# Front steps dealt out one by one to each engine, sample attention moved ahead of the last group, one choice of experts moved ahead of the front

## The chip, the cores and the metric

The kernel runs on one core of a Trainium2 chip. The metric is the device time of one execution in microseconds (us), the median of several runs. Engines: PE (TensorE, matrix products), DVE (VectorE), ACT (ScalarE), POOL (GpSimd, which issues the gathers here), SP (SyncE, which issues all other DMAs). Each engine works through its own instructions strictly in order; semaphores connect them.

## The reference

One layer over 1024 prompt tokens and 128 sample tokens (8 streams of 16), together nine tiles of 128 tokens, D = 1024:

```
h = rms_norm(x);  z = h @ w_in            # rq rk rv rg fq fk fv and forget gates
ro = retention(rq, rk, rv)                # 8 heads of 64, chunked recurrence
fo = fox attention(fq, fk, fv, logf)      # 8 heads of 64; samples also see 256 cached frames
x = x + concat(norm(ro)*silu(rg), norm(fo)) @ w_out
xn = rms_norm(x)
q = xn @ wq                               # 8 heads x 2 halves x 128
s1, s2 = q1 @ keys1, q2 @ keys2           # 128 scores each
v1,i1 = top16(s1); v2,i2 = top16(s2)
cv,ci = top16(v1[:,None] + v2[None,:])    # 16 of 256 pairs
e = i1*128 + i2;  g = softmax(cv)         # 128 experts per token (8 heads x 16)
x = x + sum(g * gelu(xn . u[e]) * v[e])   # u, v: 16384 x 1024 each
```

## The kernel before

Five programs follow one another: norm, a first projection, retention, a second projection, and the tail. Only the tail changes. It does, for each of the nine tiles of 128 tokens, 128 *gathers* (one per expert slot): gather n fetches for each of the 128 tokens a row of u and v (8 KB), 1 MB in all, into one of NR = 9 ring buffers. DVE multiplies the u half with the token's x and sums (a *dot*, L1701). After four dots DVE and ACT make the gelu weights (*weigh*, L1710 to L1723, with ACT's tanh at L1234, `gelu_tanh`), and PE adds four v halves with 16 matrix products into `yp` (*add_v*, L1458). That frees four ring buffers; POOL waits for it (`uv_free`) before it issues the next four gathers (L1068). Four dots and one add_v are a *block*; a tile has 32 blocks, the program 288. `replicate_x` on PE (L1446) and `spread_x` on ACT (L1230) copy a tile's x into the four rows of 32 that the dots read.

What a tile needs before its gathers is the *front*. The tiles go in three groups of three (g = 0, 1, 2; tile 8, the last of group 2, holds the samples). The front of a group has, in order:

- `load`: SP loads queries `fq`, keys `kTg`, values `vg`, decays `cB`, retention output `mix`
- `fox` m (24 in group 0 and 1, 16 in group 2): one head and one tile of prompt attention, scores on PE (L1275), a DVE pass (L1600), exp on ACT, transposes and values on PE; `fout` collects a pair of heads
- in group 2, sample attention: `sload` loads what it needs, `sprep` prepares on DVE, and nine rounds of `skeys`, `sscore`, `snorm` (PE L1328 to L1364, DVE L1631, L1636, ACT L1159), then `sback`
- `hload` to `hxt`: norms, the product with w_out (L1390), residual, second norm, transposes (L1400)
- `rq`, `rturn`, `rscore` i (12 per group): the product with wq (L1411), transposes (L1420), scores against the keys (L1429, semaphore `s_mm`); ACT copies each result; `rtop` i, p on DVE (L1507 to L1520) takes the top 16. Copy i of the scores on ACT waits for `top_done` of i - 2
- the *choice* of a tile, `rcand` i, p (31 pieces with work, L1527 to L1583, on DVE), then `rexp` on ACT (exp L1214, and 16 copies of the indices, L1122), `rgate` on DVE (L1691), `rmove` on ACT (16 copies of the gates). Gathers of tile t wait for its indices (`moved`).

The order of all this is fixed when the program is written. In before, `front_steps(g)` gives one list for all engines. Group 0's whole list runs before the first dot, with the choice of tile 0 after the four top-16 steps that it needs. `due_steps` spreads the lists of group 1 (behind the choices of tiles 1 and 2) and group 2 over blocks 0 to 191, by a rough cost on PE and DVE, and each engine does its share of a block's steps in that block. Gather 4 and all later ones also wait for the twelfth `rscore` of group 0 (`s_mm` 12), because the ring's buffers hold weights until then; gathers 0 to 3 do not.

The scratch area `S` is shared: in before the sample attention uses the parts that prompt attention used, so it must come after it. SP takes its share too, with the stores of y, the loads of x and `xTn` between the steps, in the same order.

## Time and profile before

| | |
|---|---|
| median of 3 runs | 4227.95 us (4224.69 to 4232.9) |
| the profiled execution | 4225.2 us, span 4223.3 us |
| first and last gather issued | 943.9 and 4202.9 us |
| moved by all DMAs | 1347.64 MB, of it 1208.03 MB by gathers |
| DVE, PE busy | 2497.4 us (59%), 2441.4 us (58%) |
| longest share of the chain that ended last | gathers, 18% of the span |

"DMA share" in the rows is how busy the 16 DMA engines were; the view shows 1.01 where they were never idle. The span falls into three parts: up to about 940 us the projections and group 0's front, then gathers beside the front of groups 1 and 2, and from about 3200 us gathers alone.

### The profile page before, as it was taken

How to read it: one execution, taken by the hardware profiler on the slowest of the kernel's cores; microseconds unless marked ns; L12 is line 12 of the kernel's file. 1: busy time of each engine (PE TensorE's matmuls, PEld its weight loads, DVE VectorE, ACT ScalarE, POOL GpSimd, SP SyncE). 2: the span in 40 equal slices, each digit the busy share in tenths (PEclk: the TensorE clock that was granted, in tenths of full speed). 3: DMA queues.
4: the chain of work that ended last, by engine and by line, in shares of the span. 5: the costliest groups of instructions: out<-in, count | busy, mean ns of one | idle time of the engine just before them, and what ended most of it. 6: DMA issues, size and time to landing. Idle time of an engine off the chain costs nothing. (4 is left out here: it accounts for less than half of the span.)

```text
span 4223.3 us, 34616 instructions
## 1 busy us (share of the span) xinstructions
PE 2441.4 (58%) x11906; PEld 1010.6 (24%) x11906; DVE 2497.4 (59%) x6235; ACT 478.1 (11%) x1311; POOL 1357.3 (32%) x1257
## 2 busy tenths in 40 slices
PE   7998996757338667533376766764334334334333
PEld 3465443323004223200033432221001001001000
DVE  3211720166956558999565454788985555555555
ACT  1000111221013111100022111111000000000000
POOL 0000220001433333444333233344444444444443
PEclk9966996778559889765588677987556556556555
DMA  3001034113999999999999799999999999999998
GB/s 107 20 10 52 20 117 151 74 40 137 415 365 387 388 386 417 403 410 411 415 415 399 303 374 394 376 405 406 420 416 418 419 416 412 419 417 418 422 418 371
DMA packets 241776, 1347.64 MB, mean 319 GB/s; under 512 B 33457, under 2 KB 47097, under 8 KB 94145
## 3 DMA queue, kind: packets, MB, share of 16 engines
q0 software_dynamic: 165888, 1208.03, 69.8%
q1 hardware_dynamic: 73408, 135.08, 8.8%
q10 hardware_dynamic: 2304, 2.32, 0.2%
q8 instruction: 94, 1.54, 0.1%
q14 instruction: 82, 0.66, 0.0%
HBM read 1318.14 MB, written 27.21 MB: 319 GB/s over the span
## 5 line engine op out<-in xcount | busy, mean ns | idle before, releaser
L1068 POOL DMA_INDIRECT M<-in_peer_uv,M x1152 | 1277.7, 1109 | 2069.8 <-PE yp L1458 1616.1
L1701 DVE SCALAR_TENSOR_TENSOR M<-M 128x1024 f32<-128x1024 f32 x1152 | 1407.3, 1225 | 650.9 <-DMA M<-in_peer_uv,M 616.9
L1458 PE MATMUL yp<-M,strips 128*32 128x512 f32 x4608 | 923.5, 945 | 1441.0 <-DVE strips L1723 1396.8
L1458 PEld LDWEIGHTS yp<-M,strips 128*32 128x32 f32 x4608 | 161.6, 147 | 2112.9 <-DVE strips L1723 1668.4
L332 PE MATMUL z<-M 128*128 128x512 f32 x1008 | 440.7, 594 | 1.4 <-PEq L104 1.0
L1234 ACT ACTIVATE gel<-gel 128x4 f32<-128x4 f32 x288 | 59.8, 208 | 1948.9 <-DVE gel L1712 1938.4
L1411 PE MATMUL ab<-M 128*128 128x512 f32 x576 | 271.0, 622 | 11.4 <-DMA M<-in_peer_wq 10.1
L332 PEld LDWEIGHTS z<-M 128*128 128x128 f32 x1008 | 189.0, 191 | 225.8 <-issue 225.8
L414 POOL TENSOR_SCALAR small<-small 128x8 f32<-128x8 f32 x27 | 6.1, 227 | 514.6 <-DVE small L483 514.6
L1411 PEld LDWEIGHTS ab<-M 128*128 128x128 f32 x576 | 111.2, 200 | 154.9 <-issue 153.3
L1600 DVE CUSTOM_DVE_ANT_0 M<-ab,M 128x896 f32<-128x896 f32 (+6 forms) x64 | 48.4, 758 | 155.9 <-PE ab L1277 88.2
L1275 PE MATMUL ab<-M 64*128 64x512 f32 (+3 forms) x192 | 97.5, 622 | 51.1 <-issue 28.3
L1723 DVE SCALAR_TENSOR_TENSOR strips<-gel,exg 128x128 f32<-128x128 f32 x288 | 84.0, 292 | 68.5 <-ACT gel L1234 59.3
L1446 PE MATMUL ef<-ident,M 128*32 128x128 f32 x2304 | 92.0, 290 | 17.3 <-issue 12.5
L1701 DVE DVE_READ_ACCUMULATOR M<-M 128x1 f32 x1152 | 95.4, 83 | 0.0
L1298 PE MATMUL d<-M 128*64 128x128 f32 x576 | 89.0, 306 | 10.9 <-ACT M L1116 10.9
L1718 DVE TENSOR_TENSOR exg<-e,gel 128x128 f32<-128x128 f32 x288 | 84.0, 292 | 10.0
L1390 PE MATMUL c<-M 128*128 128x512 f32 x144 | 75.4, 674 | 19.1 <-ACT M L1178 14.0
L1507 DVE MAX8 M<-M 128x8 f32<-128x128 f32 x144 | 31.3, 280 | 91.8 <-ACT M L1210 91.8
L1446 PEld LDWEIGHTS ef<-ident,M 128*32 128x32 f32 x2304 | 72.1, 118 | 52.0 <-issue 37.7
L1298 PEld LDWEIGHTS d<-M 128*64 128x64 f32 x576 | 70.0, 153 | 27.2 <-issue 26.6
L1429 PE MATMUL d<-M 128*128 128x128 f32 x288 | 45.1, 304 | 41.4 <-issue 22.4
(201 smaller groups left out, 2356.7 us busy)
## 6 DMA issues: line engine op xcount, KB each, us to landing
M<-in_peer_wq SPq DMA_DIRECT2D x12, 2048.0 KB, 28.5
M<-in_peer_uv,M POOLq DMA_INDIRECT x1152
M<-in_w_in SPq DMA_DIRECT2D x7, 2048.0 KB, 9.1
M<-in_w_out SPq DMA_DIRECT2D x24, 512.0 KB, 22.5
M<-in_x_prompt SPq DMA_DIRECT2D x16, 512.0 KB, 5.9
x_scratch<-M SPq DMA_DIRECT2D x9, 512.0 KB, 8.0
xts_scratch<-M SPq DMA_DIRECT2D x9, 512.0 KB, 20.9
M<-xts_scratch SPq DMA_DIRECT2D x9, 512.0 KB
```

What stands on the lines that cost most here:

```text
L332: last = nc.tensor.matmul(z[n % 3][:, :], hT[:, k, t * P:(t + 1) * P], wbuf[:, gi % 2, k, :], start=(k == 0), stop=(k == KC - 1))
L1068: nc.gpsimd.indirect_dma_start(ring[n % NR], None, a["peer_uv"], bass.IndirectOffsetOnAxis(ap=idxH[:, t % 6, s // 4, s % 4:s % 4 + 1], axis=0)
L1234: nc.scalar.activation(gel[:, n % 2, 2, :], gel[:, n % 2, 1, :], ACT.Tanh).then_inc(gel2, 1)
L1275: nc.tensor.matmul(s[:, c:c + w], fq[b0:b0 + 64, r, i * P:(i + 1) * P], kTg[b0:b0 + 64, r, c:c + w], start=True, stop=c + w < width)
L1298: last = nc.tensor.matmul(Dk[b0:b0 + 64, 0:P], vg[:, j, h * HD:(h + 1) * HD], pT[:, n % 2, j, :], start=(j == 0), stop=(j == t))
L1390: last = nc.tensor.matmul((C, Dk)[c][:, :], mT[:, t % 2, k, :], wout(g)[:, k, 512 * c:512 * c + 512], start=(k == 0), stop=(k == KC - 1))
L1411: last = nc.tensor.matmul(half_ab[i % 2], xT[:, tt, k, :], wq(g, b)[:, k, :], start=(k == 0), stop=(k == KC - 1))
L1446: last = nc.tensor.matmul(EF[32 * b:32 * b + 32, half, k * P:(k + 1) * P], xTn[:, 4 * half + k, 32 * j:32 * j + 32], ident[:, :], start=Tr ...
L1458: last = nc.tensor.matmul(yp[32 * j:32 * j + 32, 512 * c:512 * c + 512], strips[:, n % 2, j, :], ring[(4 * n + j) % NR][:, D + 512 * c:D + ...
L1701: nc.vector.scalar_tensor_tensor(out=row, in0=row, scalar=1.0, in1=xrep[:, s % 4, :], op0=ALU.mult, op1=ALU.mult, accum_out=dots[:, t % 2, ...
L1718: link(nc.vector.tensor_tensor(exg[:, :, :], bc(e32[:, :].unsqueeze(1), [P, 4, 32]), bc(g[:, 3, :].unsqueeze(2), [P, 4, 32]), ALU.mult))
L1723: nc.vector.scalar_tensor_tensor(out=strips[:, n % 2], in0=bc(g[:, 2, :].unsqueeze(2), [P, 4, 32]), scalar=1.0, in1=exg[:, :, :], op0=ALU. ...
```

## The change

`front_steps()` now gives each step its part on every engine, with a cost and the steps it must wait for, including who holds a PSUM bank. There are two lists (*threads*): all choices, and the rest. `deal` walks through time and gives each engine its next step or its next piece of expert work (dot, tanh, add_v, gather), whichever can start first; a step is placed ahead of expert work only if it ends by the time that work is ready, give or take a slack. When a choice and another step could start at once, the choice goes first. Each engine now has its own list of what stands before which dot (`due["dve"][n]`, n a dot), block (`due["pe"]`, `due["act"]`), gather (`due["pool"]`), or one of three places per tile (`due["sp"]`).

With that: group 0's steps end between the first dots, not before them. `spread` (tile 0's x) stands between the second and third `rq` of group 0. The choice of tile 1 stands in the middle of group 0's top-16 steps. `load` is split: keys, values and decays wait only for the last `rscore` of the group before, queries and `mix` (`loadq`) for the last gate. Sample attention comes before group 2's prompt attention, in parts of `S` that the scores and choices don't use; it has its own copy of the sample queries (`qs`), and `sload` waits only for group 1's last `rscore`. What is computed stays the same.

```diff
-        def front_steps(g):
-
-            nt, L = len(tiles_of(g)), FIRST[g + 1] - FIRST[g]
-            out = [(0, 0, "load", g)] + [(3.0, 0, "pad", g)] * (3 if g else 0)
-            for m in range(L + 3):
-                blocks = FOX[min(FIRST[g] + m, FIRST[g + 1] - 1)][2] + 1
-                out.append((0.7 * blocks, 0.3 + 0.13 * blocks, "fox", g, m))
-                if m >= 2 * nt + 2 and (m - 2) % (2 * nt) == 0:
-                    out.append((0.6, 0.7, "fout", g, (m - 2) // (2 * nt) - 1))
-            if nt < GT:
...
-            choice = [[(0, 1.15, "rcand", g, i, p) for p in range(CAND)] +
-                      [(0, 0, "rexp", g, i), (0, 0.6, "rgate", g, i), (0, 0, "rmove", g, i)] for i in range(GT)]
...
+
+            def add(thread, name, **parts):
+                thread.append((name, {e: (p[0], list(p[1:])) for e, p in parts.items()}))
+
+            def bank(names, engine, name):
...
+        def front_steps():
...
+            def add(thread, name, **parts):
+                thread.append((name, {e: (p[0], list(p[1:])) for e, p in parts.items()}))
...
+                chosen = [("dve", ("rgate", g - 1, GT - 1))] if g else []
+                if nt < GT:
+                    add(rest, ("sload", g), sp=(30.0, *routed))
+                    for p in range(3):
+                        add(rest, ("sprep", g, p), dve=(1.3, ("sp", ("sload", g))))
+                    for b in range(NB + 1):
+                        at = [("dve", ("snorm", g, b - 1)), ("dve", ("sscore", g, b - 1))] if b else []
+                        dead = [("pe", ("sscore", g, b - 1))] if b else []
+                        late = [("sp", ("sscore", g, b - 2))] if b >= 2 else []
+                        add(rest, ("skeys", g, b), pe=(3.2, *at, *late, ("sp", ("sload", g)), *bank("AB", "act", ("skeys", g, b))),
+                            act=(1.9, ("pe", ("skeys", g, b)), *dead))
+                        ready = [("act", ("skeys", g, b)), ("dve", ("sprep", g, 2))]
+                        ready += [("sp", ("snorm", g, b - 2))] if b >= 2 else []
+                        add(rest, ("sscore", g, b), sp=(20.0, ("pe", ("skeys", g, b))),
+                            pe=(5.0, *ready, *bank("C", "act", ("sscore", g, b))),
+                            dve=(1.0, ("pe", ("sscore", g, b))), act=(0.5, ("dve", ("sscore", g, b)), *at))
+                        add(rest, ("snorm", g, b), sp=(20.0, ("pe", ("sscore", g, b))),
+                            dve=(0.7, ("act", ("sscore", g, b)), ("pe", ("skeys", g, b))))
+                    add(rest, ("sback", g), pe=(1.2, ("dve", ("sscore", g, NB)), *bank("A", "act", ("sback", g))),
+                        act=(0.6, ("pe", ("sback", g))))
+                    routed = [("act", ("sback", g))]
+                add(rest, ("load", g), sp=(40.0 if g else 12.0, *routed))
+                add(rest, ("loadq", g), sp=(15.0, *chosen))
...
+                    if g == 0 and i == 2:
+                        add(rest, ("spread", g), pe=(5.0, ("sp", ("hxt", g, GT - 1))), act=(5.0, ("pe", ("spread", g))))
...
+                for i in range(GT):
+                    top = ("rtop", g, 4 * i + 3 if g == 0 else n - GT + i, 4)
+                    for p in range(CAND):
+                        add(choice, ("rcand", g, i, p), dve=(1.15, ("dve", top)))
+                    add(choice, ("rexp", g, i), act=(4.6, ("dve", ("rcand", g, i, CAND - 1))))
+                    add(choice, ("rgate", g, i), dve=(0.7, ("act", ("rexp", g, i))))
+                    add(choice, ("rmove", g, i), act=(4.2, ("dve", ("rgate", g, i))))
+            return choice, rest
...
-        def due_steps():
-
...
+        def deal(threads):
...
+            slack = {"pe": 2.5, "dve": 2.5, "act": 0.5, "pool": 2.0, "sp": 0.0}
+            count = {"pe": 32 * TILES, "dve": P * TILES, "act": 32 * TILES, "pool": P * TILES, "sp": 3 * TILES}
...
+            def step_start(e, th):
+                if at[e][th] == len(queue[e][th]):
+                    return None
+                need = queue[e][th][at[e][th]][1][e][1]
+                if any(d not in done for d in need):
+                    return None
+                return max([free[e]] + [done[d] + 0.1 for d in need])
...
+                if e == "pool":
+                    moved = done.get(("act", ("rexp", i // P // GT, i // P % GT)))
+                    if moved is None or i >= NR and (i - NR) // 4 >= len(freed):
+                        return None
+                    empty = done.get(("pe", ("rscore", 0, 4 * GT - 1)))
+                    if i >= 4 and empty is None:
+                        return None
+                    return max(moved, empty if i >= 4 else 0.0, freed[(i - NR) // 4] if i >= NR else 0.0)
+                if e == "dve":
+                    return None if i >= len(landed) else landed[i]
...
+            while True:
+                best = None
+                for e in engines:
+                    work = work_ready(e)
+                    bound = hoped(e) if work is None else work
+                    found = None
+                    for th in range(len(threads)):
+                        start = step_start(e, th)
+                        if start is None or found and found[0] <= start:
+                            continue
+                        cost = 0.1 if e == "sp" else queue[e][th][at[e][th]][1][e][0]
+                        if start + cost <= bound + slack[e]:
+                            found = (start, e, th)
+                    if found is None and work is not None:
+                        found = (max(work, free[e]), e, None)
+                    if found and (best is None or found[0] < best[0]):
+                        best = found
+                if best is None:
+                    break
+                start, e, th = best
+                i = did[e]
+                if th is not None:
+                    name, parts = queue[e][th][at[e][th]]
+                    at[e][th] += 1
+                    due[e][i].append(name)
+                    free[e] = start + (0.1 if e == "sp" else parts[e][0])
+                    done[(e, name)] = start + parts[e][0]
+                    continue
...
-            qbd = S[:, 0:1024].rearrange("p (r b a q) -> p r b a q", r=PAIRS, b=NB, a=2)
-            ckT = S[:, 1024:2048].rearrange("p (r n) -> p r n", r=PAIRS)
-            pn, pns = S[:, 2048:2320], S[:, 2320:2592]
-            psT = S[:, 2592:2976].rearrange("p (j m) -> p j m", j=3)
-            foT = S[:, 2976:3488].rearrange("p (r n) -> p r n", r=PAIRS)
-            kTs = S[:, 3488:4000].rearrange("p (r n) -> p r n", r=PAIRS)
-            e64 = S[0:64, 4000:5024].rearrange("p (b m) -> p b m", b=NB)
-            lfs, cs, ones_s = S[0:64, 5024:5296], S[0:64, 5296:5568], S[0:64, 5568:5840]
+            kTs = S[:, 0:512].rearrange("p (r n) -> p r n", r=PAIRS)
+            e64 = S[0:64, 512:1536].rearrange("p (b m) -> p b m", b=NB)
+            qs = S[:, 1536:2048].rearrange("p (r n) -> p r n", r=PAIRS)
+            qbd = S[:, 5904:6928].rearrange("p (r b a q) -> p r b a q", r=PAIRS, b=NB, a=2)
+            ckT = S[:, 6928:7952].rearrange("p (r n) -> p r n", r=PAIRS)
+            pn, pns = S[:, 7952:8224], S[:, 8224:8496]
+            psT = S[:, 8496:8880].rearrange("p (j m) -> p j m", j=3)
+            foT = S[:, 8880:9392].rearrange("p (r n) -> p r n", r=PAIRS)
+            lfs, cs, ones_s = S[0:64, 9392:9664], S[0:64, 9664:9936], S[0:64, 9936:10208]
...
-            due = due_steps()
+            due = deal(front_steps())
...
+                        w = (tiles_of(g)[-1] + 1) * P
                         if g:
-                            sp.wait_ge(q_mm, 4 * GT * g)
-                            sp.wait_ge(gate_done, GT * g)
-                        w, t0 = (tiles_of(g)[-1] + 1) * P, GT * g
-                        sp.dma_start(fq, a["qts"][:, :, t0 * P:(t0 + GT) * P]).then_inc(fq_in, 16)
+                            sp.wait_ge(s_mm, 4 * GT * g)
+                        if len(tiles_of(g)) < GT:
+                            sp.wait_ge(fT_ev, 1)
...
+                    elif kind == "loadq":
+                        t0 = GT * g
+                        if g:
+                            sp.wait_ge(gate_done, t0)
...
-                        sp.wait_ge(ofin, 4 * g + 4)
+                        sp.wait_ge(s_mm, 4 * GT * g)
                         sp.dma_start(kTs, a["kts"][:, :, NP_TOK:]).then_inc(sc_in, 16)
+                        sp.dma_start(qs, a["qts"][:, :, NP_TOK:]).then_inc(sc_in, 16)
...
-                for n in range(NR):
+                for n in range(P * TILES):
+                    for step in due["pool"][n]:
+                        front(step)
                     if n == 4:
                         pool.wait_ge(s_mm, 4 * GT)
                     gather(n)
-                for b in range(32 * TILES):
-                    for step in due[b]:
-                        front(step)
-                    for n in range(4 * b + NR, min(4 * b + NR + 4, P * TILES)):
-                        gather(n)

             @block.scalar
             def _(act):
...
-                for step in front_steps(0)[0]:
-                    front(step[2:])
-                dve.wait_ge(e32_in, 16)
                 for t in range(TILES):
                     for s in range(P):
+                        for step in due["dve"][t * P + s]:
+                            front(step)
+                        if t == 0 and s == 0:
+                            dve.wait_ge(e32_in, 16)
                         dot(t, s)
-                        for step in between(due[32 * t + s // 4], s % 4):
-                            front(step)
                         if s % 4 == 3:
                             weigh(t, s // 4)
                         if s == 2 and t >= 1:
                             finish(t - 1)
+                for step in due["dve"][P * TILES]:
+                    front(step)
```

DVE at the end of group 0's front, in before: the choice of tile 0 (L1581 its last piece, L1691 the gate) and the next top 16, then, after the last top (L1520), the first dot (L1701) with the choice of tile 1 (from L1527).

```order
L1581 SCALAR_TENSOR_TENSOR M<-M 128x128
L1583 TENSOR_TENSOR M<-M 128x128
L1687 TENSOR_REDUCE M<-M 128x8
L1688 RECIPROCAL small<-M 128x8
L1691 TENSOR_TENSOR gate<-M,small 128x128
L1507 MAX M<-M 128x8 x4
...
L1516 MAX M<-M 128x8 x4
L1520 MAX_INDEX M<-M 128x8 x4
L1701 SCALAR_TENSOR_TENSOR M,dots<-M 128x1024
```

The same place in the change (L1882 is the dot, L1697 and L1701 the end of a top 16, L1688 the start of one, L1708 to L1764 a choice, L1891 the weigh):

```order
L1697 MAX M<-M 128x8 x4
L1882 SCALAR_TENSOR_TENSOR M,dots<-M 128x1024
L1701 MAX_INDEX M<-M 128x8 x4
L1882 SCALAR_TENSOR_TENSOR M,dots<-M 128x1024
L1688 MAX M<-M 128x8 x4
L1882 SCALAR_TENSOR_TENSOR M,dots<-M 128x1024 x2
...
L1701 MAX_INDEX M<-M 128x8 x4
L1688 MAX M<-M 128x8 x4
L1708 CAST M<-M 128x256
...
L1762 SCALAR_TENSOR_TENSOR M<-M 128x128
L1764 TENSOR_TENSOR M<-M 128x128
L1692 MAX_INDEX M<-M 128x8
```

Dots 0 to 3 now stand around the end of the sixth top and the start of the seventh, and after the first row of top 9 (counted from 1) the whole choice of tile 1 stands before its second row.

DVE at the first dots of tile 6, in before (L1730 adds tile 5 to the output after tile 6's third dot; the first rows are the last weigh of tile 5):

```order
L1718 TENSOR_TENSOR exg<-e,gel 128x128
L1723 SCALAR_TENSOR_TENSOR strips<-gel,exg 128x128
L1701 SCALAR_TENSOR_TENSOR M,dots<-M 128x1024 x3
L1730 TENSOR_TENSOR M<-yp,M 128x1024
L1701 SCALAR_TENSOR_TENSOR M,dots<-M 128x1024
```

In the change, L1762 and L1764 are the last piece of the choice of tile 6, and L1868 to L1872 its gate:

```order
L1882 SCALAR_TENSOR_TENSOR M,dots<-M 128x1024
L1762 SCALAR_TENSOR_TENSOR M<-M 128x128
L1764 TENSOR_TENSOR M<-M 128x128
L1882 SCALAR_TENSOR_TENSOR M,dots<-M 128x1024
L1891 SCALAR_TENSOR_TENSOR gel<-dots 128x4
...
L1701 MAX_INDEX M<-M 128x8 x4
L1868 TENSOR_REDUCE M<-M 128x8
...
L1716 MAX M<-M 128x8 x8
L1882 SCALAR_TENSOR_TENSOR M,dots<-M 128x1024
```

The dot after L1764 is the last of tile 5, the one after L1716 the first of tile 6: that choice ended well before in before, by block 164 of 288, and now ends at the last dot of tile 5.

PE in a round of sample attention, in before (L1362, L1364 values, L1328 to L1336 the next `skeys`, L1458 an add_v, L1344 the next scores):

```order
L1362 MATMUL d<-M 128x32 x2
L1364 MATMUL d<-M 128x32
L1328 MATMUL ab<-ident,M 128x128 x8
L1335 MATMUL d<-ident,M 128x128 x2
L1336 MATMUL d<-ident,M 16x128
L1458 MATMUL yp<-M,strips 32x512 x8
L1344 MATMUL c<-M 128x272
```

In the change (L1641 is the add_v, L1545 and L1547 values, L1511 to L1519 `skeys`):

```order
L1545 MATMUL d<-M 128x32 x2
L1547 MATMUL d<-M 128x32
L1641 MATMUL yp<-M,strips 32x512 x8
L1511 MATMUL ab<-ident,M 128x128 x8
L1518 MATMUL d<-ident,M 128x128 x2
L1519 MATMUL d<-ident,M 16x128
L1641 MATMUL yp<-M,strips 32x512 x8
```

A round that had one add_v has two now, so it stretches over eight dots in place of four.

## Rows read from the trace of the kernel before

**Rows 1.** The page: DMA busy in 40 slices, and two of its costliest groups.

```profile
DMA  3001034113999999999999799999999999999998
...
L1701 DVE SCALAR_TENSOR_TENSOR M<-M 128x1024 f32<-128x1024 f32 x1152 | 1407.3, 1225 | 650.9 <-DMA M<-in_peer_uv,M 616.9
...
L1234 ACT ACTIVATE gel<-gel 128x4 f32<-128x4 f32 x288 | 59.8, 208 | 1948.9 <-DVE gel L1712 1938.4
```

**Rows 2.** Stretches: length, busy PE, PEld, DVE, ACT, POOL, clock, DMA share, GB/s.

```profile
940.00:1040.00 100.00, 71.75 (x452) 39.10 (x452) 62.44 (x303) 24.47 (x60) 11.39 (x11) 0.88 0.26 98
1040.00:1240.00 200.00, 64.94 (x288) 10.70 (x288) 164.14 (x385) 19.81 (x84) 85.42 (x75) 0.56 1.01 412
1240.00:1300.00 60.00, 43.50 (x201) 20.80 (x202) 29.00 (x70) 15.21 (x39) 15.85 (x16) 0.71 0.72 278
...
1430.00:1600.00 170.00, 122.02 (x449) 48.18 (x447) 97.90 (x267) 18.04 (x41) 57.05 (x54) 0.84 0.95 383
1600.00:2300.00 700.00, 373.77 (x2222) 139.51 (x2222) 545.90 (x1437) 99.37 (x283) 292.19 (x259) 0.72 1.01 413
2300.00:2480.00 180.00, 111.50 (x615) 64.17 (x614) 79.11 (x200) 21.86 (x64) 43.01 (x45) 0.62 0.84 317
2480.00:2680.00 200.00, 135.46 (x736) 57.35 (x737) 110.37 (x285) 22.25 (x50) 69.66 (x66) 0.82 0.95 380
...
3200.00:4200.00 1000.00, 378.02 (x2352) 82.78 (x2352) 585.97 (x1282) 33.30 (x122) 434.60 (x393) 0.61 1.01 418
```

**Rows 3.** Instructions in time at the first gathers: start, us, engine, what, waited for.

```profile
903.63 2.48 DVE L1531 TENSOR_TENSOR M<-M 128x1024 f32<-128x1024 f32 x2
...
938.80 0.28 DVE L1583 TENSOR_TENSOR M<-M 128x128 f32<-128x128 f32 x1
939.12 0.31 ACT L1214 ACTIVATE M<-M 128x128 f32<-128x128 f32 x1 [31.65 <-DVE M L1583]
939.34 4.28 ACT L1122 CAST M<-M 32x32 int32<-32x32 f32 x16
...
940.23 0.87 DVE L1507 MAX8 M<-M 128x8 f32<-128x128 f32 x4
...
943.64 4.30 ACT L1122 COPY M<-gate 32x32 f32<-32x32 f32 x16
...
943.92 1.21 POOL L1068 DMA_INDIRECT M<-in_peer_uv,M  x1 [100.51 <-ACT M L1122]
...
945.78 0.29 DVE L1520 FIND_INDEX8 M<-M 128x8 uint32<-128x128 f32 x1
...
948.61 1.11 PE L1420 MATMUL c<-ident,M 128*128 128x128 f32 x4 [34.89 <-ACT M L1196]
...
1013.65 2.06 PE L1446 MATMUL ef<-ident,M 128*32 128x128 f32 x56
...
1013.99 0.94 POOL L1068 DMA_INDIRECT M<-in_peer_uv,M  x1 [65.14 <-PE d L1429]
...
1028.86 0.59 ACT L1230 COPY M<-ef 128x512 f32<-128x512 f32 x1 [0.33 <-PE ef L1446]
...
1032.17 0.16 DVE L1710 SCALAR_TENSOR_TENSOR gel<-dots 128x4 f32<-128x4 f32 x1
...
1037.03 1.17 POOL L1068 DMA_INDIRECT M<-in_peer_uv,M  x1 [17.12 <-PE yp L1458]
```

**Rows 4.** Waits from 2300 to 2480 us: us in total, times, longest.

```profile
DVE mins L1631 <- PE c L1353: 33.9, 8, 5.6
DVE M L1636 <- PE d L1364: 33.3, 8, 5.7
```

**Rows 5.** Waits of DVE from 1200 to 1300 us.

```profile
DVE M L1600 <- issue: 32.2, 3, 26.3
```

**Rows 6.** DMA issues from 1200 to 1300 us: size, median us to landing.

```profile
M<-qts_scratch SPq DMA_DIRECT2D x1, 768.0 KB, 16.2
```

**Rows 7.** Waits from 2600 to 2680 us.

```profile
PE d L1429 <- issue: 14.4, 1, 14.4
```

More of the change, by code:

```diff
@@ L1249, in _ @@
                         spread_x(t + 1, 3)
+                for step in due["act"][32 * TILES]:
+                    front(step)
             @block.tensor
@@ L1475, in _ @@
                         add_v(t, k)
+                for step in due["pe"][32 * TILES]:
+                    front(step)
             @block.vector
```

360 lines of the change are left out of this document (221 added, 139 removed).

## The prediction

> **What bounds the kernel now.** I read the page first: its DMA line is low in the first quarter and nearly always 9 after, while no engine is busy for more than 59% of the span (the table above and [rows 1]). So from about 1000 us on the gathers set the time, and what can be won is time in which the DMA engines stand still, at the start or between. The view by stretches shows it [rows 2]: from 3200 us, with nothing beside the gathers, the DMA share is 1.01 at 418 GB/s, so a gather (1.05 MB) takes 2.5 us. From 1040 to 1240, where DVE is busy for 164 of 200 us with dots and the choices of tiles 1 and 2, the share is 1.01 too. From 1600 to 2300, which holds most of group 1's tops and choices and nearly all of group 2's prompt attention, the share is 1.01 again. A choice beside dots, or prompt attention beside add_v, thus costs nothing today.
>
> Idle DMA time is (1.01 - share) x length: 0.29 x 60 = 17.4 us (1240 to 1300, the start of group 1's attention), 0.06 x 170 = 10.2 us (1430 to 1600, group 1's w_out product and first scores), 0.17 x 180 = 30.6 us (2300 to 2480, sample attention), 0.06 x 200 = 12 us (2480 to 2680, the same steps of group 2 as 1430 to 1600) [rows 2]. Together 70.2 us. The remaining stretches are at full share. The loads of the front move the same bytes before and after but for 256 KB, so they cancel.
>
> Then I read the instructions in time around the first gathers [rows 3]. The choice of tile 0 takes DVE from 903.63 to 939.1 us. PE waits 34.89 us for it, until 948.6. Four gathers go at 943.92, the fifth at 1013.99 (it waits for the twelfth score), the tenth at 1037.03 (it waits for the first add_v, which waits for `spread`).
>
> **The start.** Three things move.
>
> (a) `spread` now stands before the third score. In before it runs from 1013.65 to about 1029 us, 15 us with gaps [rows 3]; it can't be less than its eight ACT copies of 0.59 us, about 5. All before gather 0 moves back by that. I take 12, nearer to the row: the choice of tile 0 ends at 939.1 + 12 = 951.
>
> (b) DVE then has, before the rest of top 9: tops 5 to 8, each 5.8 us (940.23 to 946.07 for one [rows 3]), a gate 0.8, four dots of 1.225 + 0.08 us [rows 1], a weigh of about 1, and a fifth of top 9, 31.4 us in all, to 982.5. PE and ACT keep up, for in the change two more scores and a wq product fall into the time in which PE waits today.
>
> (c) Then comes the whole choice of tile 1, 35.5 us, to 1018. Nobody needs it before gather 128. But the last score waits for the eleventh copy on ACT, this for top 9, and that now stands behind the choice: rest of top 9 4.9, a piece of top 10 and the gate 1.7 (1024.6), ACT's copies of the gates 4.3 us [rows 3], which stand ahead of the last transposed copy, then 0.6 and 1.2 for copy and score: gather 4 goes at about 1031, 17 us later than now. In return add_v 0 is long done, so gathers 4 to 12 follow at once, where before gather 9 waited until 1037. From 940 to 1040 the DMAs moved 98 x 100 us = 9.8 MB [rows 2]; now 4.2 MB by gathers 0 to 3, and from 1032.5 at 412 GB/s another 3.1 MB, 7.3 MB. The 2.5 MB missing are 6 us. With 6 us for `spread` it would be 0. At the other end, if PE did nothing useful in its wait and the 15 and 35.5 us came on top of 1014, gather 4 would go at 1065: 5.6 MB less than before at 1040, and 10 MB missed by 1065, 38 us. Value taken: +6.
>
> **Group 1's attention.** In before DVE waited up to 26.3 us before the first pass, with dots queued behind it [rows 5]; PE's first score waited for loads issued only at 1206, after the last gate. In the change keys, values and decays are loaded 130 us ahead; only the queries (768 KB) follow the last gate, at dot 52, and DVE's first pass is before dot 59, seven gathers or 17.5 us later. The queries took 16.2 us to land among those loads [rows 6]. So at most a few us of wait: I leave 3 of the 17.4 us. The Trainium skill (DMA: Bandwidth & Descriptors, section Queues, rings and completion order) says that each DMA engine takes packets from its queues in turn; queries then get about half the rate, and land sooner than behind the nine gathers on their way. By a first-come order those 9 MB would take 22 us and the hole would be about 8 us in place of 3; the 16.2 us don't decide between the two.
>
> **Product and scores of groups 1 and 2.** PE waits there, once 14.4 us before a score, for nothing that the view names [rows 7]; the score's only other condition is its keys, so I read it as a load that is late. The distance from load to use grows (w_out: two blocks to twelve dots; wq to the first score of group 2: four blocks to six), while the same 4 MB of weights must land beside the gathers. I leave 6 of 10.2 and 6 of 12 us.
>
> **Sample attention.** In before DVE stands in eight rounds 33.9 + 33.3 us for PE, 8.4 us a round, with dots queued behind it [rows 4]. Everything of a round sat in one block. Now a round has eight dots (20 us at 2.5 us a gather), and the scores, the division and the copy of the values stand between dots, so that a good part of PE's and ACT's time passes under dots. Bounds: nothing hidden: 8 dots of 1.31, two weighs, 1.6 us of its own and 8.4 us of wait are 22.5 us, 2.5 us over, 9 rounds 22 us; all hidden: 0. The ring holds nine gathers and so evens out a wait of a few us. I leave 6 of the 30.6 us. The vectors and caches are loaded from group 1's last score on, 140 dots ahead.
>
> Group 2's attention has 20 blocks for what took 16 at full share, so nothing there.
>
> **A new hole at tile 6.** Group 2 is later by about 115 dots: its first choice ends before dot 767, the last of tile 5, and gather 768 needs its indices. So the ring runs empty: after gather 767 lands come the dot 1.3, the first two gelu operations 0.3, tanh 0.2 [rows 1], the last two copies of `spread` 1.2, exp 0.3 and the 16 index copies 4.3, then the gather's issue 0.9 [rows 3]: 8.5 us, and half a us to first data. DMA stands idle for 9 us. If the dots were late already it's less (0 at the least), at most 22.5 (nine empty buffers).
>
> **SP's queue.** Loads for x and `xTn` now stand behind front steps, at worst `xTn` of tile 6 behind group 2's last transposes, at dot 650, while PE wants it at dot 752. Nothing.
>
> **The sum.** 4225.2 (the profiled execution; span 4223.3) - 70.2 (all holes) + 3 + 6 + 6 + 6 (what is left of them) + 9 (tile 6) + 6 (start) = 4191.0. The profiled execution is 2.8 us under the median of before and inside the spread of its three runs, so I keep 4191 for the median; of the 34 us about 3 are within what runs differ by.
>
> **The rivals.**
>
> *Everything fits:* the holes vanish (5 us left), `spread` costs 6 and the start nothing: 4225.2 - 70.2 + 5 + 9 = 4169. For it: full share wherever load and use were apart. Against: PE's granted clock in the sample rounds, 0.62 on the mean, nearer to its lower level of 1.2 GHz (0.5) than to 2.4 [rows 2].
>
> *The waits stay, only further apart:* samples leave 22 us, products and scores their whole 22.2, group 1's start 5, tile 6 9, start 9: 4225.2 - 70.2 + 67 = 4222, no change or barely faster. For it: every engine is in order, and DVE's wait for PE still stands before a dot. Against: the ring's 22 us.
>
> *Choice first (slower):* the rule that a choice wins a tie bites at both ends. At the start PE gains nothing under the first choice, 38 us; at tile 6 the whole ring must refill, 22.5; with 21 us of old holes left: 4225.2 - 70.2 + 21 + 38 + 22.5 = 4236. It decides from the point where start and tile 6 cost over 49 us. Against: scores 5 to 7 have no wait on the choice.
>
> *The change doesn't do what it says:* sample attention starts only after the last choice of group 1 (dot 423), close to where it was (about 450), so it may win nothing by its place; that is within the second rival.
>
> **How the numbers follow.** Forecast (4178 to 4205) 0.5, all fits 0.2, waits stay 0.2, choice first 0.1. A run within 0.2% (8.5 us) of 4228 is what a measurement can't tell from no change. Of "waits stay" 0.1 lies there, 0.07 is faster, 0.03 slower; of "choice first" 0.07 is slower and 0.03 within. Faster 0.77, same 0.13, slower 0.10. The range 4164 to 4226 takes in the second rival and leaves out the slower end.
>
> **What would show it.** Gather 4 at 1025 to 1035 us, right behind the choice of tile 1 (right), or beyond 1050 (choice first). Ten gathers without a gap then. DMA share 1.0 in group 1's attention. In the sample rounds DVE waits for PE of under 3 us each. One idle stretch of DMA of 8 to 12 us right before tile 6's first dot, ended by ACT's index copies. It is wrong if the DMA share outside of it is below 0.95 over a hundred us anywhere after 1040, or if the last gather goes less than 20 us earlier than 4202.9.

## The result, and the profile after

The changed kernel takes 4164.8 us (median of 4 runs, 4160.1 to 4168.0), the kernel before 4230.4 us beside it (4 runs). The ratio is 0.9843, 95% interval 0.9825 to 0.9862: 65.6 us faster. The forecast was 4191, the range 4164 to 4226; the gain was 66 us where I had put 34, almost as in the rival *Everything fits* (4169), and outside of the forecast's own 4178 to 4205. It lies 0.8 us inside of the range's lower end.

The page of the kernel after: the DMA line, the chain that ended last (the gathers have 35% of it, before 18%), and the group of the dots, as in [rows 1].

```profile
DMA  3001034101999999999999999999998999999998
...
DMA M<-in_peer_uv,M 35%; PE yp L1641 11%; POOL M L1256 7%; DVE M L1882 6%; PE ef L1629 1%; DMA M<-qts_scratch 1%; PE ab L1594 1%; DVE strips L1904 1%; DVE exg L1899 1%; PE c L1573 1%; PE d L1573 1%; PE d L1480 1%; PE ab L1457 1%; DVE gel L1
...
L1882 DVE SCALAR_TENSOR_TENSOR M<-M 128x1024 f32<-128x1024 f32 x1152 | 1410.0, 1225 | 867.7 <-DMA M<-in_peer_uv,M 840.9
```

DVE's dots wait longer for gathers now (840.9 us, before 616.9). That is the gain itself: the dots are in time more often, and the DMAs set the pace. By stretches, as [rows 2]:

```profile
940.00:1040.00 100.00, 43.35 (x143) 21.81 (x141) 90.05 (x351) 25.51 (x83) 12.15 (x13) 0.72 0.20 78
1040.00:1240.00 200.00, 87.83 (x399) 26.91 (x400) 150.95 (x361) 23.85 (x81) 82.75 (x72) 0.62 1.02 419
1240.00:1300.00 60.00, 44.10 (x232) 21.00 (x231) 40.39 (x93) 14.29 (x38) 22.98 (x23) 0.79 1.01 419
1300.00:1430.00 130.00, 86.08 (x684) 42.73 (x683) 81.77 (x184) 28.79 (x74) 59.91 (x53) 0.82 0.99 404
1430.00:1600.00 170.00, 96.61 (x376) 33.35 (x374) 95.05 (x199) 12.45 (x32) 69.56 (x62) 0.75 1.02 419
1600.00:2300.00 700.00, 371.11 (x2118) 138.48 (x2118) 549.59 (x1516) 75.30 (x243) 289.45 (x256) 0.71 1.01 409
2300.00:2480.00 180.00, 102.11 (x713) 49.09 (x713) 94.61 (x217) 20.85 (x56) 66.95 (x58) 0.67 0.96 390
2480.00:2680.00 200.00, 136.09 (x717) 63.49 (x713) 127.48 (x281) 38.98 (x90) 87.14 (x78) 0.78 1.01 419
2680.00:3160.00 480.00, 302.15 (x1564) 115.26 (x1560) 347.73 (x973) 44.00 (x108) 195.42 (x172) 0.79 1.00 412
3160.00:3180.00 20.00, 5.10 (x138) 3.32 (x128) 17.93 (x66) 10.93 (x39) 9.18 (x8) 0.73 0.49 191
...
3200.00:4100.00 900.00, 331.87 (x1932) 69.73 (x1928) 588.16 (x1332) 42.66 (x171) 400.35 (x356) 0.61 1.01 418
```

Two stretches of the kernel before that [rows 2] left out:

```profile
1300.00:1430.00 130.00, 93.77 (x788) 52.38 (x787) 85.22 (x197) 40.18 (x102) 53.58 (x49) 0.91 1.01 412
...
2680.00:3200.00 520.00, 243.54 (x1281) 72.68 (x1279) 443.70 (x1221) 54.50 (x184) 224.05 (x199) 0.71 1.01 413
```

Both kernels move the same bytes, within 0.3 MB, so the right measure of a hole is missing bytes: (418 - GB/s) / 418 x length, 418 being the rate with nothing beside the gathers. In us:

| stretch | before | after |
|---|---|---|
| 1040 to 1240 | 2.9 | -0.5 |
| 1240 to 1300 | 20.1 | -0.1 |
| 1300 to 1430 | 1.9 | 4.4 |
| 1430 to 1600 | 14.2 | -0.4 |
| 1600 to 2300 | 8.4 | 15.1 |
| 2300 to 2480 | 43.5 | 12.1 |
| 2480 to 2680 | 18.2 | -0.5 |
| 2680 to 3200 | 6.2 | 6.9 + 10.9 (3160 to 3180) |
| sum | 115.4 | 47.9 |

The difference is 67.5 us. Less the 4.8 us that the start costs (78 for 98 GB/s over 100 us), it is 62.7; the spans differ by 65.0.

The same stretch doesn't hold the same steps in both kernels. In after group 1's scores run from 1620 us, the sample rounds from 2199 to 2378, group 2's prompt attention from 2442, its w_out product from 2712 to 2800 and its scores behind that. The rates by these places:

```profile
1600.00:1840.00 240.00, 173.19 (x924) 73.26 (x928) 187.49 (x628) 28.99 (x66) 97.31 (x85) 0.85 1.00 407
...
2199.00:2378.00 179.00, 119.88 (x680) 64.15 (x680) 103.62 (x250) 17.87 (x62) 74.74 (x65) 0.66 0.99 404
...
2442.00:2680.00 238.00, 165.35 (x984) 78.20 (x988) 148.82 (x327) 50.54 (x113) 97.83 (x88) 0.77 0.99 407
2680.00:2800.00 120.00, 78.38 (x352) 28.23 (x345) 68.05 (x145) 7.35 (x20) 50.12 (x45) 0.80 1.01 420
2800.00:3160.00 360.00, 223.77 (x1213) 87.03 (x1215) 279.68 (x829) 36.65 (x88) 145.30 (x128) 0.79 1.00 409
```

The gathers in time, at the start and at tile 6 (start, us, engine, what, waited for), to set beside [rows 3]:

```profile
951.01 1.21 POOL L1256 DMA_INDIRECT M<-in_peer_uv,M  x1 [107.92 <-ACT M L1305]
...
957.82 1.11 PE L1603 MATMUL c<-ident,M 128*128 128x128 f32 x4 [16.92 <-ACT M L1380]
...
1021.56 1.12 PE L1603 MATMUL c<-ident,M 128*128 128x128 f32 x4 [20.43 <-ACT M L1380]
...
1029.45 0.94 POOL L1256 DMA_INDIRECT M<-in_peer_uv,M  x1 [73.49 <-PE d L1612]
...
3168.69 0.94 POOL L1256 DMA_INDIRECT M<-in_peer_uv,M  x1 [17.01 <-ACT M L1305]
```

PE stood still twice, behind the choices of tile 0 and tile 1; gather 4 went at 1029.45 us; gather 768, the first of tile 6, waited for its indices.

### The profile page after: what moved, and what is told of

The parts are those of the page before. It is cut to its first block, busy times and chain, and to the rows that moved or that the text cites. A ratio compares the mean times of both kernels' runs of the same rounds, so it can differ in the third digit from the quotient of the medians.

```text
span 4158.3 us, 34613 instructions
## 1 busy us (share of the span) xinstructions
PE 2454.2 (59%) x11906; PEld 1026.4 (25%) x11906; DVE 2505.9 (60%) x6235; ACT 474.4 (11%) x1311; POOL 1387.2 (33%) x1257
## 4 chain that ended last, share of the span: by engine, by line
DMA 37%; PE 18%; DVE 14%; POOL 7%; issue 5%; SPq 1%; ACT 1%; another core or an unknown queue 0%; POOLq 0%; DVEq 0%; ACTq 0%
DMA M<-in_peer_uv,M 35%; PE yp L1641 11%; POOL M L1256 7%; DVE M L1882 6%; PE ef L1629 1%; DMA M<-qts_scratch 1%; PE ab L1594 1%; DVE strips L1904 1%; DVE exg L1899 1%; PE c L1573 1%; PE d L1573 1%; PE d L1480 1%; PE ab L1457 1%; DVE gel L1891 1%; DVE gel L1893 1%
## 5 line engine op out<-in xcount | busy, mean ns | idle before, releaser
L1256 POOL DMA_INDIRECT M<-in_peer_uv,M x1152 | 1306.5, 1134 | 1975.4 <-PE yp L1641 1491.3
L1882 DVE SCALAR_TENSOR_TENSOR M<-M 128x1024 f32<-128x1024 f32 x1152 | 1410.0, 1225 | 867.7 <-DMA M<-in_peer_uv,M 840.9
L1641 PE MATMUL yp<-M,strips 128*32 128x512 f32 x4608 | 929.4, 949 | 1387.3 <-DVE strips L1904 1331.1
L1641 PEld LDWEIGHTS yp<-M,strips 128*32 128x32 f32 x4608 | 162.3, 148 | 2018.1 <-DVE strips L1904 1555.6
L1480 PE MATMUL d<-M 128*64 128x128 f32 x576 | 97.9, 327 | 1.3 <-ACT M L1299 1.3
L1470 PE MATMUL c<-ident,M 128*128 128x128 f32 x288 | 62.7, 337 | 59.0 <-ACT M L1291 53.2
L1882 DVE DVE_READ_ACCUMULATOR M<-M 128x1 f32 x1152 | 95.0, 82 | 0.0
L1278 ACT ACTIVATE M<-M,mins 128x896 f32<-128x896 f32 (+6 forms) x64 | 49.6, 775 | 207.2 <-DVE mins L1780 207.0
```

Of the source, the lines that this page charges most:

```text
L1256: nc.gpsimd.indirect_dma_start(ring[n % NR], None, a["peer_uv"], bass.IndirectOffsetOnAxis(ap=idxH[:, t % 6, s // 4, s % 4:s % 4 + 1], axis=0)
L1470: last = nc.tensor.transpose(four(C)[:, j % 4, :], pr[:, n % 3, j * P:(j + 1) * P], ident[:, :])
L1480: last = nc.tensor.matmul(Dk[b0:b0 + 64, 0:P], vg[:, j, h * HD:(h + 1) * HD], pT[:, n % 2, j, :], start=(j == 0), stop=(j == t))
L1641: last = nc.tensor.matmul(yp[32 * j:32 * j + 32, 512 * c:512 * c + 512], strips[:, n % 2, j, :], ring[(4 * n + j) % NR][:, D + 512 * c:D + ...
L1882: nc.vector.scalar_tensor_tensor(out=row, in0=row, scalar=1.0, in1=xrep[:, s % 4, :], op0=ALU.mult, op1=ALU.mult, accum_out=dots[:, t % 2, ...
```

## The experiments

Theory: the gain is gather rate won back in the front's stretches, because a step stands between dots where it is ready and its loads are issued earlier; the rule that a choice wins a tie costs at the start and at tile 6. Rivals: the sample attention's new place does it; the split of the load does it; the holes only moved. The runs were made on three occasions, each with the kernel before beside them, whose median was 4229.0, 4230.0 and 4222.3 us. After itself was timed only with the result, not beside them, so a difference to it is given by the medians, and by the ratios to before where these say otherwise. Some us of such a difference lie ahead of any edit: gather 0 was issued between 950.75 and 956.94 us in the profiled kernels whose start is planned as in after.

### Two parts made alone in the kernel before

```diff
-                    out += [(2.5, 0, "skeys", g, b), (4.0, 1.0, "sscore", g, b), (0, 0.8, "snorm", g, b)]
+                    out += [(6.0, 0, "skeys", g, b), (8.0, 1.0, "sscore", g, b), (3.0, 0, "pad", g), (0, 0.8, "snorm", g, b)]
```

> The kernel before, and only the costs of the sample attention's steps in its rough plan raised, so that its nine rounds stand 2.1 blocks apart (blocks 112 to 129) where they stood about one block apart (114 to 121); the order of the steps stays. My theory: most of what the change won lies in the sample stretch, where the kernel before moved 317 GB/s for 180 us and lost some 43 us by bytes, because one round's chain of waits (PE, DVE, ACT, PE) is longer than the block it stands in. Spreading alone should then give back half or more: ratio to before 0.992 to 0.996, 18 to 32 us. Rival A, the sample attention's small-row loads are what holds the gathers' rate, so that spacing changes nothing: 0.999 to 1.001. Rival B, each round costs a fixed stall wherever it stands, since before puts steps behind a dot and not where they are ready: 0.998 to 1.003, with the same total deficit over a longer stretch.

Measured 4208.9 us, 0.9952 (0.9934 to 0.9970), 20 us. In 2300 to 2480 the rate went from 317 [rows 2] to:

```profile
2300.00:2480.00 180.00, 102.96 (x659) 53.09 (x663) 99.61 (x243) 17.06 (x56) 63.82 (x60) 0.66 0.97 391
```

So the short distance between the rounds held the rate there. DVE's waits for PE in the rounds fell from 67.2 to 32.8 us (2300 to 2530). The rounds' loads were spread with them, so this run alone doesn't clear the small rows; *What a small row costs* does. By bytes 32 us were won in this stretch and 7 in 2480 to 2680; 1600 to 2300 (413 to 407 GB/s) and 2680 to 3200 (413 to 405) gave back 10 each. The plan leaves the group's other steps fewer blocks now; that this is the reason is not shown.

The early load:

```diff
+            due[0].insert(0, ("loadk", 1))
+            due[62].insert(0, ("loadk", 2))
...
-                    if kind == "load":
+                    if kind == "loadk" or kind == "load" and g == 0:
                         if g:
-                            sp.wait_ge(q_mm, 4 * GT * g)
-                            sp.wait_ge(gate_done, GT * g)
+                            sp.wait_ge(s_mm, 4 * GT * g)
...
```

> The kernel before, with one part of the change alone: keys, values and decays of groups 1 and 2 are loaded early (they wait only for the last score of the group before; placed ahead of block 0 and block 62), queries and mix stay behind the last gate. My theory: it takes away the wait of the first prompt scores of a group, which left 8.9 us of holes by DMA share in 1240 to 1300 and some part of the 10.2 us in 1430 to 1600: ratio 0.995 to 0.9975, 10 to 20 us faster. Rival A, the queries land last in any case and the wait stays: 0.999 to 1.001. Rival B, the early load takes rate from gathers at the start where the DMA is full, or SP is held in front of its other loads: 1.001 to 1.004.

Measured 4200.1 us, 0.9937 (0.9921 to 0.9952), 29 us, above my span.

```profile
940.00:1040.00 100.00, 72.58 (x452) 39.12 (x452) 61.55 (x300) 24.77 (x61) 9.85 (x11) 0.86 0.36 139
...
1240.00:1300.00 60.00, 50.90 (x295) 27.56 (x294) 39.13 (x96) 22.68 (x60) 21.11 (x21) 0.90 0.95 380
```

In 1240 to 1300, the stretch that I had named, it is 14.6 us by bytes (380 for 278 GB/s), more than the 8.9 us that I had put there (by [rows 2] the share makes 17.4). What I had not seen stands in the first row: 139 for 98 GB/s over 100 us, 4.1 MB of loads that now run while the DMAs are idle before the gathers, 9.8 us. The change as made doesn't get that: its start has 78 GB/s.

Both together:

> The kernel before with both parts that were made alone: the early load of keys, values and decays (alone 0.9937) and the nine sample rounds 2.1 blocks apart (alone 0.9952). My theory: they act in different stretches, so they add: ratio 0.988 to 0.990, some 45 to 50 us, about three quarters of what the whole change gave, with a plan that is still the rough one in blocks. Rival: both take from the same holes (the ring is only so deep, what one gives back the other already had): 0.992 to 0.994.

Measured 4180.0 us, 0.9894 (0.9874 to 0.9915), 50 us: 29 and 20 add up. These two parts, in the old plan by blocks, give three quarters of the change's 66 us. They act by the mechanisms of the change, but are not its exact parts (the load in after starts later). The last quarter was made alone in no run.

### Parts taken back from the kernel after

The load of group 1 behind the last gate again:

```diff
                         if g:
                             sp.wait_ge(s_mm, 4 * GT * g)
+                        if g == 1:
+                            sp.wait_ge(gate_done, GT)
```

> The kernel after, with the split of the load undone for group 1: keys, values and decays wait for the last gate again, as the queries do; the order of all instructions is unchanged. In the kernel before, the early load alone gave 29 us (4228.95 to 4200.13). My theory, that the early load is worth much only because the first prompt scores stood in front of the gathers' own work on PE: here the scores of group 1 stand at about the same dot, so it costs 14 to 25 us, ratio to before 0.988 to 0.991. Rival, the dealt order has put enough of the tile's add_v work ahead that the ring absorbs the wait: 0.984 to 0.986, no change to after.

Measured 4184.2 us, 0.9894 (0.9875 to 0.9912), 19 us slower than after. Its waits from 1040 to 1240 us, and the stretch at fault:

```profile
POOL M L1258 <- PE yp L1643: 103.6, 16, 30.6
...
PEld ab L1459 <- DMA M<-qts_scratch: 29.1, 1, 29.1
```

```profile
1200.00:1220.00 20.00, 14.00 (x35) 4.87 (x35) 8.12 (x19) 3.44 (x8) 3.75 (x4) 0.50 0.40 140
1220.00:1240.00 20.00, 16.57 (x88) 8.30 (x88) 14.33 (x33) 4.82 (x13) 7.63 (x7) 0.76 0.95 363
```

PE stood 29.1 us at the first score of group 1, with the add_v that frees the ring queued behind it, and the gathers stopped for lack of buffers: 15.9 us by bytes. Another 6 us of the profiled executions' difference lie at the start (gather 0 at 956.94 us, in after 951.01), where the edit does nothing. The ring absorbs part of such a wait, not all; the rival falls.

The sample attention behind the prompt attention again (its load waits `ofin`, `hload` waits `fT_ev`):

```diff
-                    add(rest, ("sload", g), sp=(30.0, *routed))
+                    add(rest, ("sload", g), sp=(30.0, full))
...
-                    routed = [("act", ("sback", g))]
+                    full = ("act", ("sback", g))
```

> The kernel after, with the sample attention behind the last group's prompt attention again (its load waits for the last prompt head, the rest of the front for its result), in the new scratch places; all dealt engine by engine by the same rules. Its nine rounds stand between dots 533 and 595 (after: 430 and 491), so as far apart as in after. My theory: the gain comes from the dealing (a step stands where it is ready), not from the place: ratio to before 0.983 to 0.987, within 10 us of after's 0.984. Rival, the place beside the choices is what hides the rounds (the choices fill DVE while PE waits) : the sample stretch loses its 40 us again, 0.992 to 0.995.

Measured 4168.1 us, 0.9862 (0.9845 to 0.9880), 3 us over after by the medians, 8 by the ratios, and the intervals overlap. The place beside the choices is worth nothing that I can measure; the distance between rounds is. DVE's wait in the eight rounds, 67.2 us in [rows 4], is this in after (2200 to 2370 us), 2.2 us a round:

```profile
DVE M L1817 <- PE d L1547: 17.9, 5, 5.6
```

### The rule for ties

```diff
+            def rest_first(e):
+                step = queue[e][0][at[e][0]][0]
+                t = GT * step[1] + step[2]
+                return not (t and P * t - did["dve"] < 80)
...
-                        if start is None or found and found[0] <= start:
+                        if start is None:
                             continue
+                        if found and (found[0] < start or found[0] == start and not rest_first(e)):
+                            continue
```

> The kernel after, with one rule of the deal changed: when a choice and another step could start at once, the choice goes first only where its tile's gathers come within 80 dots (never for tile 0); otherwise the other step does. The planned places: choices of tiles 1 and 2 end at dots 31 and 76 (after: 4 and 46), those of tiles 6 to 8 at 745, 802, 846 (after: 767, 803, 853), the sample rounds at 373 to 433 (after: 430 to 491). My theory, that the rule costs after its start (PE stood still 16.9 and 20.4 us behind the two choices; gather 4 at 1029.45) and its hole at tile 6 (10.4 us by share): gather 4 near 990 to 1000, no hole at 3160 to 3180, so 35 to 48 us faster than after, ratio to before 0.973 to 0.976 (4116 to 4129 us). Rival A, the start is won and the ring then runs into choices of tiles 1 and 2 that come too late: a hole near gather 128 of 15 to 30 us, ratio 0.979 to 0.982. Rival B, with choice and sample rounds interleaved DVE is late and the holes come back at 1900 to 2200 us: 0.980 to 0.986.

Measured 4124.6 us, 0.9759 (0.9744 to 0.9774), 40 us faster than after by the medians, 36 by the ratios, and the best kernel of all. The start and tile 6:

```profile
983.84 1.21 POOL L1264 DMA_INDIRECT M<-in_peer_uv,M  x1 [137.35 <-ACT M L1313]
...
1007.92 0.94 POOL L1264 DMA_INDIRECT M<-in_peer_uv,M  x1 [18.83 <-PE d L1620]
```

```profile
3160.00:3180.00 20.00, 6.34 (x32) 0.99 (x24) 16.45 (x52) 0.21 (x1) 8.11 (x8) 0.67 1.02 423
```

Gather 4 goes 21.5 us earlier than in after (I had said 30 to 40), and the hole at tile 6 is gone. By bytes the start gave 21 us (167 GB/s in 940 to 1040, in after 78) and tile 6 its 11. To split the 40 us, the same rule from tile 3 on (`return not (t < 3 or P * t - did["dve"] < 80)`), and at tiles 0 to 2 alone (`return not (t > 2 or t and P * t - did["dve"] < 80)`):

> The kernel after, with the changed tie rule (the choice first only where its gathers come within 80 dots) from tile 3 on alone; the start, tiles 0 to 2, is planned as in after. Choices of tiles 6 to 8 end at dots 725, 775, 819 (after: 767, 803, 853), sample rounds at 324 to 396. Both places together gave 40 us (4124.6 against 4164.8). My theory: tile 6's hole is 10 us by DMA share and the other 30 us are the start: 4150 to 4157 us, ratio 0.981 to 0.983. Rival, the shift of the front by some 35 dots, and not the start, gives most of it: 4125 to 4140, 0.975 to 0.979. Second rival, with sample rounds and choices of tiles 3 and 4 interleaved DVE is late: 4160 to 4170.

> The kernel after, with the changed tie rule at tiles 0 to 2 alone (choice_waits_turn had it everywhere, tie_from_tile3 from tile 3 on, and gained 40 and 16 us on after). The choices of tiles 6 to 8 end at dots 768, 803, 853, so tile 6's gathers wait as in after. My theory: the two places add, so this gives 40 less 16: 4138 to 4145 us, ratio 0.979 to 0.981, gather 4 near 1008 us, and the hole at 3160 to 3180 is there again. Rival, the later choices of group 0 push the whole front back (sample rounds at dots 460 to 516), so tile 6's hole grows by 10 us or more: 4150 to 4158.

Measured 4148.4 us, 0.9813 (0.9794 to 0.9831), 16 us faster than after by the medians, 13 by the ratios; and 4168.9 us, 0.9878 (0.9857 to 0.9899), no gain on after but a loss, 4 us by the medians and 15 by the ratios. They don't add: 16 and -4 alone, 40 together (by the ratios 13, -15 and 36). The mechanism of the second run's rival held, at a time over its 4150 to 4158. The trace of the start alone shows where its gain went. Gather 4 goes at 1008.26 there, but at tile 6:

```profile
3175.27 0.94 POOL L1264 DMA_INDIRECT M<-in_peer_uv,M  x1 [35.70 <-ACT M L1313]
```

```profile
3130.00:3190.00 60.00, 15.22 (x240) 7.26 (x240) 56.30 (x149) 12.98 (x44) 15.87 (x13) 0.64 0.50 200
```

POOL is ready for gather 768 at 3139.6 us (3175.27 - 35.70), 12 us earlier than in after (3151.7), but the indices come 6.6 us later: group 2's front ends later, since its steps, too, stand behind later choices (by the plan the sample rounds stand at dots 460 to 516 for 430 to 491). The hole is 31 us by bytes, in after 12 over the same 60 us. Over 2680 to 3200 the rate is 383 GB/s (404 in after), 26 us lost against 21 won at the start (166 for 78). Group 2's front is a second path of its own, and what is won ahead of it is lost at its end, unless the front ends earlier too, as in choice_waits_turn (dot 745 for 768).

Last, tile 0's choice first again, tile 1's put off (`return not (t < 1 or t > 2 and P * t - did["dve"] < 80 or t < 3 and P * t - did["dve"] < 123.5)`):

> The kernel after, with the tie rule changed as in the run before for tiles 3 to 8, tile 0's choice first as in after, and tile 1's choice put off behind group 0's other steps while its gathers are over 123 dots away (tie rule again). Gathers 0 to 3 are issued near 951 us as in after (choice_waits_turn: 984), and gather 4 no longer waits behind tile 1's choice. My theory: PE still loses the 17 us behind tile 0's choice, so gather 4 comes near 1010, as in choice_waits_turn, but four gathers (4 MB, 10 us) are already in: 4112 to 4122 us, ratio 0.973 to 0.975, the best so far. Rival: what counts is when gather 4 and those behind it can start, the first four only stand finished in the ring; then 4122 to 4130, no better than choice_waits_turn.

Measured 4129.6 us, 0.9767 (0.9749 to 0.9785). Gathers 0 to 3 were issued from 953.00 us on for 983.84, gather 4 at 1006.52, and it gained nothing on choice_waits_turn: the rival held. What the start is worth is told by the gathers behind gather 4.

### What a small row costs

```diff
-                        sp.dma_start(kTs, a["kts"][:, :, NP_TOK:]).then_inc(sc_in, 16)
-                        sp.dma_start(qs, a["qts"][:, :, NP_TOK:]).then_inc(sc_in, 16)
+                        for c in range(0, P, 16):
+                            t0 = NP_TOK + c
+                            sp.dma_start(kTs[:, :, c:c + 16], a["kts"][:, :, t0:t0 + 16]).then_inc(sc_in, 16)
+                            sp.dma_start(qs[:, :, c:c + 16], a["qts"][:, :, t0:t0 + 16]).then_inc(sc_in, 16)
```

> The kernel after, with the two loads of the sample's keys and queries (128 tokens, rows of 512 bytes, 1024 rows together) cut into eight loads each of 16 tokens (rows of 64 bytes, 8192 rows together): the same 512 KB with eight times the rows. In after's trace the DMA engines are never idle from 1840 to 1880 us, while these and the other small loads run, but they move 366 GB/s there, and 419 on either side, 5 us of gathers. My theory: the share of busy time does not count what small rows cost, a row costs some 0.05 to 0.06 us of one of the 16 engines whatever its size: the 7168 rows more take 22 to 27 us of the 16 engines together. The dip grows from 40 to some 90 us at a share of 1.0 or more, and the kernel is 20 us slower: 4182 to 4190 us, ratio 0.988 to 0.990. Rival A, the rate is held by what those engines move in bytes, and the dip came from something else (the caches, HBM): no change, 0.983 to 0.986. Rival B, the rows cost what I say but in the shade of the full ring, a third of it reaches the end: 0.985 to 0.987.

Measured 4175.6 us, 0.9898 (0.9880 to 0.9917): by the medians 11 us over after, by the ratios 23, since the kernel before ran 8 us faster beside it; I say 11 to 23. SP's queue from 1830 to 1900 us (packets, MB, share of 16 engines), in after and then here:

```profile
q1 hardware_dynamic: 2814, 3.72, 16.1%
```

```profile
q1 hardware_dynamic: 10240, 3.74, 23.2%
```

7426 more packets for the same bytes took 7.1% of 70 us of 16 engines, 10.7 ns of one engine each, not my 50 to 60. That is 5 us of the 16 engines; that the ratio fell into my range all the same was luck. The rest is again a wait on PE, for the cache keys that SP loads behind the small rows. What a small row costs there is its turn. From 1830 to 1840 us, with the rows cut, the engines took about one packet of SP's queue for each of the gathers', however small:

```profile
q0 software_dynamic: 567, 4.12, 99.2%
q1 hardware_dynamic: 524, 0.03, 3.7%
```

That went on until the gathers ran out; from 1870 to 1880 us 6174 of SP's packets passed. The prediction had left open whether the queues take turns (*Group 1's attention*); here they do. The wait in after:

```profile
1872.76 1.57 PEld L1511 LDWEIGHTS ab<-ident,M 128*128 128x128 f32 x8 [20.09 <-DMA M<-in_cache_fox_k]
```

and with the rows cut, in the waits from 1850 to 1900 us:

```profile
POOL M L1258 <- PE yp L1643: 36.9, 2, 32.9
PEld ab L1513 <- DMA M<-in_cache_fox_k: 34.3, 1, 34.3
```

## Why the prediction was right or wrong

**What bounds it, and the mechanism: right.** DMA idle time was the time to be won, and earlier loads and rounds between dots won it.

**The size of the holes: wrong, and the main error.** The step is "Idle DMA time is (1.01 - share) x length", with "The remaining stretches are at full share" behind it. It made 70.2 us; missing bytes make 115.4 [rows 2, and the table above]. The largest miss in one stretch is the sample stretch, 30.6 us by share and 43.5 by bytes (share 0.84, but 317 GB/s, 0.76 of 418). Its queues (packets, MB, share of 16 engines), in before:

```profile
q0 software_dynamic: 6321, 46.02, 64.9%
q1 hardware_dynamic: 5764, 10.91, 18.9%
```

SP's 10.91 MB took 34 us of the 16 engines, where 418 GB/s needs 26: 8 us. A gather's packet took 296 ns of an engine, in 3200 to 4100 us 282: 6 us. With the idle 30.6 that is about the whole 43.5. And stretches with share 1.01 ran at 412 or 413 GB/s, which over 1550 us is 19 us that I counted as nothing. Why a gather's packet lasts longer there is open: the small rows' own 10.7 ns each are far from enough.

**What is left of them: too much by share, about right by bytes.** I left 21 us outside of tile 6. By bytes 37 remain (47.9 - 10.9). By the places where the steps now stand, the two w_out products have none (419 and 420 GB/s) and the stretches with the scores 14 (407 and 409), where I left 12 for both; the sample rounds have 6 (404), as I left. What I put at nothing are 6 in group 2's prompt attention (2442 to 2680, 407), whose queries took 43.3 us to land (PE waited 4.1 us for them), 5 beside the loads for the samples (1840 to 1880) and 4 in 1300 to 1430. What in the score stretches costs the 14 was not tested. The two errors, 45 us too small before and 16 too small after, make 29 of the 31 us by which the gain of the profiled executions (65.0) was underrated.

**Group 1's attention: right.** 3 us left, none measured; the queries landed in 15.7 us (forecast from 16.2). after_late_load shows that the split of the load does it.

**The start: right in size.** Gather 4 at 1029.45 us (1031), choice of tile 1 ended at 1015.5 (1018), cost 4.8 us (6), then gathers 4 to 12 without a gap, nine, as reckoned and not the ten of *What would show it*. Within it `spread` took 7.3 us and not 12. PE's waits of 16.9 and 20.4 us behind the choices were what *Choice first* priced; they cost little beside before, but choice_waits_turn shows that they were there to be won, if tile 6 is served too.

**Tile 6: right in size** (10.9 us by bytes, 9 forecast), ended by ACT's copies as told. What I didn't see is that it ties the start to the front: costed apart, start and tile 6 would have been added, and they don't add.

**Sample attention: right mechanism, undersized.** DVE's waits are 2.2 us a round (under 3 forecast). What was too small is the hole before, not what is left. Its place, with the earlier loads that the new scratch allows, is worth 3 to 8 us at the most, within the noise; I had left that open.

**SP's queue: nothing, right.** No wait for x or `xTn` shows in the groups that wait longest. The last gather went at 4137.95 us, 65 before the old one.

## What to carry to other kernels

Where DMA is the bound, size a hole by missing bytes against the rate of an undisturbed stretch, not by the idle share, and compare step with step where the steps have moved. An in-order wait costs what exceeds the transfers still on their way when the issuing engine stops. That is less than the ring: here some four gathers, 10 to 11 us, of nine, 22.6 us, and POOL's 30.6 us behind PE's wait of 29.1 cost 16 to 19, not 8. So place each instruction that waits for a DMA at least that load's landing time behind its issue. Before crediting a gain at the start, look for the next place where a second path must be done (here the first tile of group 2): the gain stops there unless that path is moved too.

## What the runs showed of the hardware

The same PE wait costs little or much by what is on its way: 20.1 us for the cache keys in after left the DMA engines busy all through; 29.1 us in after_late_load made a hole of 15.9 us, and with 34.3 us in small_rows_cut POOL stood still for 32.9. When POOL stopped, only some four of the ring's nine gathers were still on their way: 4.6 MB came in from 1184 to 1206 us in after_late_load (beside 3.5 MB of SP's loads), 4.1 MB from 1859 to 1869 us in small_rows_cut, then none. The other buffers had landed and waited for PE. A 64-byte row costs some 11 ns of one DMA engine (10.7 over the 70 us, 11.3 beside full-rate gathers), but takes its turn like a gather's packet of some 7 KB. And a full share can hide a low rate; this is after while SP's loads for the samples landed:

```profile
1840.00:1880.00 40.00, 11.35 (x56) 3.08 (x48) 27.66 (x83) 1.69 (x5) 10.71 (x10) 0.54 1.02 366
```

A gather's packet took 316 ns of an engine there, undisturbed 282. Which of the loads does that is open.
